# Attention: K pages spread over 48 of the 64 units, V pages of the second group at every other unit

## The reference, cut to what matters

```
s = einsum('bqhmd,bkhmd->bhmqk', qi, k) * ATTN_SCALE      # causal, m = 2 maps
p = softmax(s);  attn = p[..., 0, :, :] - lam * p[..., 1, :, :]
o = einsum('bhqk,bkhe->bqhe', attn, v)
```

## Time and profile before

| | |
|---|---|
| time, median of 3 runs (lowest, highest) | 3827.69 us (3826.16, 3839.68) |
| profiled execution: time, span | 3840.46 us, 3838.6 us |
| PE, DVE, ACT, POOL busy, share of the span | 87%, 53%, 37%, 46% |
| mean granted clock of PE, share of full speed | 0.926 |
| K page loads, V page loads in the phase | 64 and 64 of 512 KB; landing 4.4 and 5.7 us (median) |

### The profile page before, as it was taken

How to read it: one execution, slowest core, us unless ns; L and a number is a source line. 1 busy time by engine, 2 the same in 40 slices (tenths; PEclk the granted TensorE clock), 3 DMA queues, 4 the chain that set the end, 5 groups by cost and what they waited for, 6 DMA issues and landing times. The chain is left out here.

```text
span 3838.6 us, 78812 instructions
## 1 busy us (share of the span) xinstructions
PE 3352.3 (87%) x34057; PEld 3083.8 (80%) x34057; DVE 2029.4 (53%) x2239; ACT 1419.6 (37%) x2233; POOL 1755.0 (46%) x724
## 2 busy tenths in 40 slices
PE   5999968999896199999999999766886999999997
PEld 2887857888886199999999999644554999999997
DVE  2956544554542664673372442199844747732722
ACT  1333323344332133433333344344554333333433
POOL 0665511000000066666656666455501666566564
PEclk8999978999997599999999999887897999999998
DMA  5555533434321454445444466666844444454442
GB/s 204 150 182 164 169 126 105 155 108 136 116 94 52 155 155 139 141 121 148 141 136 141 142 204 186 182 201 232 317 160 143 142 135 142 121 147 143 135 139 87
DMA packets 784517, 575.26 MB, mean 150 GB/s; under 512 B 45306, under 2 KB 747666, under 8 KB 783916
## 3 DMA queue, kind: packets, MB, share of 16 engines
q1 hardware_dynamic: 725686, 502.02, 43.0%
q10 hardware_dynamic: 58486, 68.20, 5.4%
HBM read 499.86 MB, written 70.29 MB: 149 GB/s over the span
## 5 line engine op out<-in xcount | busy, mean ns | idle before, releaser
L1638 POOL TENSOR_TENSOR dense_w_lo<-dense_w_raw,dense_w_hi 128x1024 fp32r<-128x1024 f32 x504 | 1279.9, 2546 | 903.1 <-ACT dense_w_hi L1721 902.9
L1690 PE MATMUL acc<-dense_x_hi,dense_w_hi 128*128 128x344 f32 x2496 | 798.9, 324 | 79.0 <-DVE dense_x_lo L1827 41.1
L1691 PE MATMUL acc<-dense_x_lo,dense_w_hi 128*128 128x344 f32 x2496 | 792.7, 322 | 0.0
L1721 ACT ACTIVATE dense_w_hi<-dense_w_raw 128x1024 fp32r<-128x1024 f32 x504 | 530.9, 1056 | 567.9 <-PE acc L1695 478.7
L1690 PEld LDWEIGHTS acc<-dense_x_hi,dense_w_hi 128*128 128x128 f32 x2496 | 474.3, 190 | 88.9 <-issue 71.9
L1690 PE MATMUL acc<-dense_hid_hi,dense_w_hi 128*128 128x344 f32 x1536 | 485.7, 321 | 0.0
L1691 PE MATMUL acc<-dense_hid_lo,dense_w_hi 128*128 128x344 f32 x1536 | 483.4, 319 | 0.0
L1691 PEld LDWEIGHTS acc<-dense_x_lo,dense_w_hi 128*128 128x128 f32 x2496 | 474.6, 190 | 1.0
L1695 PE MATMUL acc<-dense_x_hi,dense_w_lo 128*128 128x344 f32 x2496 | 447.5, 322 | 3.4 <-POOL dense_w_lo L1638 3.4
L1695 PEld LDWEIGHTS acc<-dense_x_hi,dense_w_lo 128*128 128x128 f32 x2496 | 407.2, 189 | 4.5 <-POOL dense_w_lo L1638 4.5
L745 POOL TENSOR_TENSOR x0T<-nT,levels 128x512 f32<-128x512 f32 x16 | 29.7, 1856 | 593.9 <-DVE bR L1244 593.9
(11 more groups left out here) (399 smaller groups left out, 6155.9 us busy)
## 6 DMA issues: line engine op xcount, KB each, us to landing
dense_w_raw<-in_ffn_w SPq DMA_DIRECT2D x384, 512.0 KB, 4.2
ada_quarter<-in_ada_w SPq DMA_DIRECT2D x40, 1024.0 KB, 11.2
proj_w_raw<-in_a_w_rkv SPq DMA_DIRECT2D x72, 512.0 KB, 4.6
att_k_page<-in_cache_k SPq DMA_DIRECT2D x64, 512.0 KB, 4.4
att_v_page<-in_cache_v SPq DMA_DIRECT2D x64, 512.0 KB, 5.7
scratch_mix<-proj_stage ACTq DMA_DIRECT2D x72, 344.0 KB, 2.8
scratch_mix<-dense_stage ACTq DMA_DIRECT2D x72, 172.0 KB, 2.1
dense_w_raw<-in_a_w_o SPq DMA_DIRECT2D x24, 512.0 KB, 4.4
```

The source lines that it names most:

```text
L1638: nc.gpsimd.tensor_tensor(wlo[:, i % NW], raw[:, i % NRAW], whi[:, i % NW].bitcast(F32), ALU.subtract).then_inc(S("lo"), 1)
L1690: T_.matmul(out, whi[:, s % NW, k, :], a, start=j.first and k == 0, stop=False)
L1691: T_.matmul(out, whi[:, s % NW, k, :], b, start=False, stop=False)
L1721: A(whi[:, i % NW], raw[:, i % NRAW], ACT.Copy).then_inc(S("hi"), 1)
```

## The change

Two constants and one function. `pages_of` gives four pages per three units instead of three per two: units 0 to 47 hold the 64 pages, where units 0 to 42 did, and two pages fall in the units with u % 3 = 2 instead of the odd ones. `SM` goes from units 22 and 43 to 24 and 48. `VU` goes to units 30, 34, 38, 42 for the first group (all two later) and to 53, 55, 57, 59 for the second (before 49, 52, 55, 58).

```
-        SM, VU = (22, 43), (28, 32, 36, 40, 49, 52, 55, 58)
+        SM, VU = (24, 48), (30, 34, 38, 42, 53, 55, 57, 59)
...
         def pages_of(u):
 
-            return range(min(NPAGE, 3 * u // 2), min(NPAGE, 3 * (u + 1) // 2))
+            return range(min(NPAGE, 4 * u // 3), min(NPAGE, 4 * (u + 1) // 3))
```

## The result

The changed kernel took 3838.33 us (median of 20 runs, 3827.74 to 3852.66), the kernel before 3827.45 us beside it (20 runs, 3814.17 to 3840.81): a ratio of 1.0023 with a 95% interval of 1.0013 to 1.0033, or +8.8 us (+5.0 to +12.6); the medians lie 10.9 us apart, the means 9.2. The forecast was +4.3 us, 3832, with a range of 3820 to 3845 and 0.91 on "within 0.5%".

What follows compares the result with a forecast made beforehand. DVE was taken to bound units 1 to 42, PE the units after the pages. Terms -3.8, +2.2, -1.8 and +7.7 sum to +4.3 us on the median 3827.69, so 3832 us; range 3820 to 3845.

Steps and rivals of the forecast that it cites:

- Pages in units 1 to 42: Units 1 to 42: fewer page sums, changed holds of DVE by POOL products; -3.8 us, ends -8.5 and +1.
- First group's V steps: Units 28 to 42: V steps at new places stall DVE, old waits go; +2.2 us, from -5.5 to +9.
- the term of one hold taken off: First group's V steps: a product ending during a stall holds nobody afterwards; 1.9 us taken off.
- Units 43 to 47: Seven pages come in, the second group's turning leaves, DVE ends last; -1.8 us, ends -4 and +1.
- PE alone: Units 43 to 47: the end of the range where only PE sets the length; -4 us.
- Units 48 to 62: Tail paced by PE: turning comes in, V steps stand elsewhere around waits for ACT; +7.7 us, +3 to +11.
- a gap of about 4 us in unit 53 ahead of the V matmuls: Unit 53: sign of being right, PE's gap before the V matmuls; about 4 us.
- the turning that comes in: Units 48 to 62: turning the second group's scores and weights on PE counts in full; 6.2 us.
- the cover that is lost: Unit 53: V step from unit 52 no longer stands ahead of PE's wait for ACT; +3.0 us.
- V pages late: Second group's V steps wait for page loads two units apart; 3837 to 3845 us, chance 0.2.
- The first stretch gains in full: Units 1 to 42: holds unchanged, PE's slack takes the V steps; total -7.5 us, 3820, chance 0.2.
- Nothing moves: Attention phase: DVE's work is only spread; -2 to +2 us, 3826 to 3830, chance 0.1.

Runs made afterwards that it cites:

- e3: Kernel before with only the second group's part: softmax at unit 48, V steps at 53, 55, 57, 59; ratio 1.0009 to the kernel before.
- e4: Kernel before with one V step moved from unit 52 to 53; ratio 1.0013 to the kernel before.
- e7: Kernel before with second group's V steps at units 48, 52, 56, 60 and the samples' last steps one unit later; ratio 1.0004.
- e2: Changed kernel with the first group's V steps at units 32, 36, 40, 44; ratio 1.0019 to the kernel before.
- e5: Changed kernel with each query row's load issued six pages earlier; ratio 1.0028 to the kernel before.
- e1: Kernel before with only the first group's V steps moved, to units 30, 34, 38, 42; ratio 1.0040 to the kernel before.
- e10: Kernel before with all page sums behind the unit's combine on DVE; ratio 0.9990 to the kernel before.
- e12: Changed kernel with double pages only in odd units, sums after combine, V steps at 32, 36, 40, 44, 53, 56, 58, 60, last steps one unit later; ratio 0.9978.
- e6: Kernel before with POOL multiplying only the first half of each K page's columns; 3809.39 us, one run.
- e8: Changed kernel with first group's V steps at 32, 36, 40, 44 and two pages only in odd units, eight per six; ratio 1.0000.
- e9: Kernel before with the page sum ahead of the maxima in even (long) units on DVE; ratio 1.0002 to the kernel before.

## Why the prediction was right, and where its terms were not

The direction, the class and the range were right, the size half of the timed one. In the tail the work that moved in was paid, as forecast, though the wait priced at 3.0 us opened by less than half of that. The near hit in the first stretch is luck: two errors that cancel.

*Pages in units 1 to 42: forecast -3.8, end -8.5.* By the forecast's own terms -4.5 of this fall up to unit 28; measured are -6.7 there, so it was under-sized. The failing step is that the hold of a negated maximum was counted behind second pages alone. In the kernel before the negated maxima sum to 29.17 us in 42 units, so 29.17 - 42 x 0.17 = 22.0 us of hold. Behind second pages stand 10.8 of them, as forecast ("hold 0.5 us on average", 21 x 0.5 = 10.5). Another 8.0 stand in odd units, where a product let go by a first page runs on into the next unit, and 3.2 in units 26 and 42 under POOL's squaring of the output (L2161); both were put at nothing. After the change they sum to 21.83, a hold of 14.7 us. That the step gave just this for after (7 x 0.5 + 7 x 1.6) is luck: only 10.1 of them stand behind second pages, 5.2 in the seven odd units priced at 11.2. The forecast had the hold rise by 4.2 us; in these two traces it fell by 7.3. The trace before is a high one here, too: e3, e4 and e7, with the same pages, have holds of 22.2, 17.2 and 15.1 us, e2 and e5, with the new ones, 15.9 and 14.1. So the size of the fall is uncertain, but a rise by 4 is excluded. Rows of the negated maxima and the page sums in units 1 to 28, before:

```profile
2489.32:2684.93 195.61, 19.42 (x28) 0.79 0.66 217
...
2489.32:2684.93 195.61, 50.83 (x43) 0.79 0.66 217
```

and after:

```profile
2482.36:2670.15 187.79, 14.60 (x28) 0.78 0.64 214
...
2482.36:2670.15 187.79, 44.81 (x38) 0.78 0.64 214
```

-4.8 and -6.0 (five sums fewer). The combines stay (65.26 to 65.74), and 3.7 us are lost to two steps that the forecast had not looked at: the first group's softmax, moved with `SM` from unit 22 to 24, now falls under POOL's work, its first step under the squaring of the output, its second under the K product that follows at 2653.18. These two instructions in unit 26 took 0.15 and 0.75 us before:

```profile
2651.33 1.89 POOL L2161 TENSOR_TENSOR att_o_sq<-att_o 128x1024 f32<-128x1024 f32 x1 [7.57 <-DVE att_scores L2359]
2651.40 1.83 DVE L2395 TENSOR_TENSOR att_page_weight<-att_page_weight,att_cm 64x1 f32<-64x1 f32 x1
2653.27 2.82 DVE L2397 TENSOR_SCALAR att_page_probs<-att_page_probs,att_page_weight 64x1025 f32<-64x1025 f32 x1
```

The mechanism itself shows in unit 9, whose short maxima end long before the product does, which runs from 2529.83 to 2532.17 (compare, where the same instruction takes 0.82 us):

```profile
2529.61 0.41 DVE L2340 TENSOR_REDUCE att_max<-acc 128x2 f32<-128x256 f32 x1
2530.05 2.15 DVE L2342 TENSOR_SCALAR att_neg_max<-att_max 128x2 f32<-128x2 f32 x1
```

*First group's V steps: forecast +2.2, ends -5.5 and +9.* e1 measures them alone at +10.1 in units 29 to 42, beyond the upper end. The steps of units 30, 34 and 38, forecast at 6.4 us of stalls, came out at 12.6 in the changed kernel; the waits that go (5.5) were as forecast. The failing step is that the burst was counted as 5.4 us alone: the column step one unit on, named at 1.9 us but left out of the sum, stalls DVE too, by 3.38 us in unit 32 and 1.74 in unit 40. The first stalls, "5.4 less the lead and the mean slack of 2.0", were 2.67, 2.98 and 1.81 us for 2.6, 1.2 and 2.6: near in sum, but in unit 35 the slack wasn't there at all (5.4 less the lead of 2.2 is 3.2). The step of unit 42, forecast at 3.2 us, shows as 4.58 us in e1 and 4.88 in e5, ahead of unit 43; in the changed kernel DVE's wait for POOL stands in its place. What softens it is the term of one hold taken off, 1.9 us: DVE is busy 5.8 us less, of which two sums fewer are 2.4. How much of the remaining 3.4 belongs to the stalls and how much to the pages isn't separated; in e1, with the old pages, DVE is busy 4.2 us less than before, but in e7, with the old steps, 4.6.

*Units 43 to 47: forecast -1.8, ends -4 and +1.* Measured -3.7, near "PE alone" though DVE is busy 27.78 of 30.58 us, against 32.5 forecast.

*Units 48 to 62: forecast +7.7, ends +3 and +11.* Measured +8.1, and +8.1 to +13.6 in the five traces with the new tail steps. Its named sign, a gap of about 4 us in unit 53 ahead of the V matmuls, was there in part: 1.83 + 1.34 us, of which 0.43 + 1.34 stood there before. e3 bears out the turning that comes in. For the cover that is lost e4 gives +3.7 for 3.0, but the size is a better hit than the step: the waits in unit 53 were to grow by 3.0 us and grew by 1.0 to 1.4, and the rest came with a lower clock that had not been foreseen. e3 less e4 leaves 6.8 us for the rest of the sum, forecast at 4.7, if the parts add.

*Rivals.* "V pages late" is out: no V matmul of the changed kernel waits for a load, and those that did in five other kernels waited 0.7 to 1.7 us. "The first stretch gains in full" fell by the V steps, not by the pages. "Nothing moves" is outside the interval of +5.0 to +12.6 us. Of the signs named as right, negated maxima of 1.4 us and more came in two of the seven odd units (9 and 27), and the combines in units 43 to 45 took 1.0 to 1.7 us, not 2 to 3. Of the signs named as wrong, "DVE waiting for PE in many units before 43" did appear, 10 times and 15.2 us against 4 times and 7.7.

What stays open: e8 and e9 are some 5 to 6 us shorter in the trace than before (against before's mean) and even in time. One trace of the first stretch scatters by 4 us, and the intervals are some 6 us to either side; whether more than scatter is in it, these runs can't tell.

## What to carry to other kernels

Price an instruction by what it releases on another engine and whom that holds there, not by its own length: a page here is 1.2 us of sum and up to two more of somebody else's, and e10 and e12 shortened the first stretch by choosing who. Count every operation that such a product can meet, not only the one that the page was put behind. A burst on the engine ahead is paid out of the lead at that place, and by its second half a unit later; slack averaged over a stretch may not be there, as in unit 35. Before moving work into a stretch, read which engine ends last there: in the PE-bound tail the work that came in was paid, and a burst that no longer stood ahead of a wait cost 3.7 us.

## What was not expected of the hardware

The hold by a POOL product isn't a matter of an instruction's size: a 64x1 tensor_tensor took 1.83 us instead of 0.15 (under the squaring of L2161), a 2-column negation 2.15 instead of 0.17 (under a K product), while page sums (1.20 to 1.22 us) and maxima from PSUM (2.27 to 2.29 us over 2048 columns) kept their length in all runs. In all 14 traces every held negation of units 1 to 42, some 300 in all, ends within 0.06 us of the end of a POOL product or squaring. The Trainium skill, page "GPSIMD Engine Reference", section on specifications, says that GpSimd shares its SBUF interfaces with VectorE and names two cases of contention, a 2-port performance mode and two SBUF inputs. The trace agrees for the combine, which has two SBUF inputs; what makes the 2-column negation with its one input wait, no run here shows.

Sixteen V matmuls took 3.46 us at a granted clock of 0.56 behind two gaps of 1.83 and 1.34 us, and 1.92 us a moment later. A gap can so cost more than its own length: in e4's tail PE's idle time grew by 0.8 us and its busy time by 2.9. It isn't always paid: e6's tail had PE busy 1.4 us longer at a clock of 0.91 and took the same 96.13 us.
